# Second stack: last layer 256 columns wide, rotary swap by VectorE shuffle, a gate's minimum taken ahead of its tanh

## The reference, cut to what matters

```
def _hybrid_layer(h, pos, ...):
    proj = h @ w_in                       # 2048 -> 5120
    (c_val, c_glu, c_gate, q, k, v, a_gate, r_x, r_gate) = jnp.split(proj, split_pts, axis=-1)
    c = c_val * sigmoid(c_glu)
    c = causal_depthwise_conv(c, 31 taps); c = silu(layer_norm(c)); c = c @ conv_pw_w + b
    y_conv = c * silu(c_gate)
    q = partial_rotary(q.reshape(B, L, 16, 64), pos)     # 16 heads, first 16 of 64 features
    k = partial_rotary(k.reshape(B, L, 4, 64), pos)      # 4 key heads, 4 query heads for each
    att = sliding_window_sink_attention(q, k, v, sinks)  # window 128, meta keys always seen
    y_attn = att * silu(a_gate)
    r = causal_depthwise_conv(r_x, 4 taps)
    r = rg_lru(r, ...)      # a = exp(-8 sigmoid(r @ wa + ba) softplus(-lam)), scan over tokens
    y_lru = r * silu(r_gate)
    mixed = concatenate([y_conv, y_attn, y_lru]) @ w_out  # 2048 -> 2048
    return layer_norm(alpha * h + mixed)

def _partial_rotary(x, pos):              # half = 8
    rot = concatenate([x1 * cos - x2 * sin, x2 * cos + x1 * sin])
    return concatenate([rot, x[..., 16:]])

second_block: h = layer_norm(concat(meta, x)); two layers; return h[:, 16:]
```

## Time and profile before

| | |
|---|---|
| median of 3 runs | 3391.97 us (3391.57 to 3392.92) |
| profiled execution | 3391.2 us, span 3389.4 us |
| granted TensorE clock, mean | 0.992 |
| busy share of the span | PE 98%, PEld 84%, DVE 58%, ACT 49%, POOL 15% |
| second stack | from about 2457 us to the end; first product of layer 0 at 2485.39 us, of layer 1 at 2932.64 us |

### The profile page before, as it was taken

How to read it: one execution, slowest core, us unless ns; L and a number is a source line. 1 busy time by engine, 2 the same in 40 slices (tenths; PEclk the granted TensorE clock), 3 DMA queues, 4 the chain that set the end, 5 groups by cost and what they waited for, 6 DMA issues and landing times.

```text
span 3389.4 us, 48369 instructions
## 1 busy us (share of the span) xinstructions
PE 3319.6 (98%) x17528; PEld 2838.2 (84%) x17528; DVE 1966.8 (58%) x2190; ACT 1653.5 (49%) x2322; POOL 498.9 (15%) x425
## 2 busy tenths in 40 slices
PE   8999999999999999999999999999979999999998
PEld 7888888888888888888888888888869889898897
DVE  6666645444444556666545444445466776667755
ACT  5444555555444444444555554444335464545643
POOL 4554400000000104554200000000020000010000
PEclk9999999999999999999999999999989999999998
DMA  6555555555555555555554555555533334443342
GB/s 235 173 169 175 183 174 167 168 173 173 193 192 193 199 182 182 170 173 174 175 177 165 169 173 187 193 193 185 180 138 134 116 125 156 156 138 124 124 144 95
DMA packets 157148, 567.24 MB, mean 167 GB/s; under 512 B 17536, under 2 KB 19728, under 8 KB 156752
## 3 DMA queue, kind: packets, MB, share of 16 engines
q1 hardware_dynamic: 155680, 558.00, 49.0%
q0 software_dynamic: 1344, 7.49, 0.6%
HBM read 563.32 MB, written 2.10 MB: 167 GB/s over the span
## 4 chain that ended last, share of the span: by engine, by line
PE 95%; DVE 3%; ACT 1%; POOL 1%; issue 0%; DMA 0%; SPq 0%; ACTq 0%; DVEq 0%; POOLq 0%
PE acc L1506 22%; PE acc L1508 22%; PE acc L1507 22%; PE acc L1757 6%; PE acc L1759 6%; PE acc L1758 6%; PE work L1566 1%; DVE w_lo L965 1%; PE work L1592 1%; PE work L1835 1%; PE work L1836 1%; PE work L1806 1%; PE work L1736 1%; PE work L1737 1%; PE work L1738 1%
## 5 line engine op out<-in xcount | busy, mean ns | idle before, releaser
L965 DVE TENSOR_TENSOR w_lo<-raw,w_hi 128x1024 fp32r<-128x1024 f32 x1056 | 1401.3, 1336 | 1214.4 <-ACT w_hi L565 944.0
L565 ACT ACTIVATE w_hi<-raw 128x1024 fp32r<-128x1024 f32 x832 | 876.4, 1058 | 964.3 <-PE acc L1508 961.9
L1506 PE MATMUL acc<-w_hi,hT_hi 128*128 128x512 f32 x2560 | 1015.2, 397 | 2.3 <-DVE hT_lo L971 2.3
L1508 PE MATMUL acc<-w_hi,hT_lo 128*128 128x512 f32 x2560 | 998.9, 390 | 0.0
L1507 PE MATMUL acc<-w_lo,hT_hi 128*128 128x512 f32 x2560 | 997.5, 390 | 0.0
L1508 PEld LDWEIGHTS acc<-w_hi,hT_lo 128*128 128x128 f32 x2560 | 481.0, 188 | 102.7
L1506 PEld LDWEIGHTS acc<-w_hi,hT_hi 128*128 128x128 f32 x2560 | 481.5, 188 | 97.8 <-issue 2.7
L1507 PEld LDWEIGHTS acc<-w_lo,hT_hi 128*128 128x128 f32 x2560 | 481.8, 188 | 95.8
L579 ACT ACTIVATE w_hi<-raw 128x1024 fp32r<-128x1024 f32 x224 | 236.1, 1056 | 395.8 <-PE acc L1759 381.0
L1757 PE MATMUL acc<-h_hi,w_hi 128*128 128x272 f32 x1152 | 344.7, 299 | 0.0
L1759 PE MATMUL acc<-h_hi,w_lo 128*128 128x272 f32 x1152 | 333.2, 289 | 0.0
(11 more groups left out here) (311 smaller groups left out, 3738.7 us busy)
## 6 DMA issues: line engine op xcount, KB each, us to landing
raw<-weights SPq DMA_DIRECT2D x1056, 512.0 KB, 3.3
mat<-mats POOLq DMA_DIRECT2D x2, 1536.0 KB, 8.1
X<-x_in SPq DMA_DIRECT2D x8, 256.0 KB, 7.9
out<-out_rows SPq DMA_DIRECT2D x8, 256.0 KB, 2.3
par<-params POOLq DMA_DIRECT2D x2, 640.0 KB, 5.4
cst<-consts POOLq DMA_DIRECT2D x1, 872.0 KB, 5.0
cst<-consts POOLq DMA_DIRECT2D x1, 704.0 KB, 4.8
ropeC<-rope POOLq DMA_DIRECT2D x2, 256.0 KB, 5.6
```

The source lines that it names most:

```text
L565: act.activation(w_hi[:, slot, :], raw[:, slot, :], ACT.Copy).then_inc(hi_ready, 1)
L965: dve.tensor_tensor(w_lo[:, s % RING, :], raw[:, s % RING, :], w_hi[:, s % RING, :], ALU.subtract)\
L1506: pe.matmul(o, stat[0][:, kc, token], hi, start=(kc == 0), stop=False)
L1508: ins = pe.matmul(o, stat[1][:, kc, token], hi, start=False, stop=(kc == KC - 1))
```

## The change

1. **Last layer.** `FROM[l]` is 0 for layer 0 and 16 for the last. In the last layer the query tiles, `r_gate`, `a_gate` and `c_gate` tiles (24 of 40), all 16 output tiles and what ACT, DVE, POOL and PE make of them skip the 16 meta columns: 256 instead of 272. Keys, values, the convolution's input and the recurrent part keep 272. The meta tokens' own scores, softmax parts and transposes fall away (`score_parts`).
2. **Rotary swap.** `turn_keys` and `rotate` are gone. DVE swaps features by `stream_shuffle`, which permutes partitions within groups of 32 (`PAIR`); the sign sits in the sine table. Query heads are reordered on the host (`head_pairs`), with the gate columns, output rows and sinks, so that a pair's two heads use the two key heads that already lie on the two halves of a key tile. Keys are now made in one go: a shuffle and three operations of 2 x 272 columns, after g = 14. `turn_values` no longer waits for the keys; the first `scores` does.
3. **Order.** `values` moves from `at` = 6 to `at` = 0 of the next period, directly ahead of `scores`; `copy_o` moves to `at` = 5, ahead of `exps`. `lru_min` runs after g = 44, 48, 52, 56, first in its list, and no longer waits for the tanh; the tanh of b = 0 waits for the minimum instead, and heads ACT's list of its half. `short_conv` stands ahead of the taps of its half.
4. The constants lose the five 128-column matrices: 552 KB in place of 872.

The diff, cut to its core (the left-out lines put `k:TOK` or `FROM[l]:TOK` in place of all columns, and count semaphores anew):

```diff
-E_ID, E_ROT, E_SEL, E_SELROT = 0, P, 2 * P, 4 * P
-E_COS = 6 * P
+FROM = [0] * (DEPTH - 1) + [META]
+PAIR = [i + 8 if i < 8 else i - 8 if i < 16 else i for i in range(32)]
+E_ID = 0
+E_COS = P
...
-        def conv_tap(eng, ch, j):
+        def conv_tap(eng, l, ch, j):
             x, o = PJ[:, CVAL + ch, :], PJ[:, CGLU + ch, :]
             w = R2_DW + CONV_K * ch + CONV_K - 1 - j
+            k = max(j, FROM[l])
             if j == 0:
-                return eng.tensor_scalar(o, x, par2[:, w:w + 1], par2[:, R2_DWB + ch:R2_DWB + ch + 1], ALU.mult, ALU.add)
-            return eng.scalar_tensor_tensor(o[:, j:TOK], x[:, 0:TOK - j], par2[:, w:w + 1], o[:, j:TOK], ALU.mult, ALU.add)
+                return eng.tensor_scalar(o[:, k:TOK], x[:, k:TOK], par2[:, w:w + 1], par2[:, R2_DWB + ch:R2_DWB + ch + 1],
+                                         ALU.mult, ALU.add)
...
+        def of_tokens(l, i):
+            return FROM[l] if QUERY <= i < QUERY + 8 or i >= RGATE else 0
+        def score_parts(l):
+            return ((P, S1, S0), (P, S0, SMETA)) + (() if FROM[l] else ((META, SMETA, S_COLS),))
...
                 act.wait_ge(gate_ready2, 8 * l + n + 1)
                 j, b = n // 2, n % 2
+                if b == 0:
+                    act.wait_ge(gate_min, 4 * l + j + 1)
                 dst = (PJ[:, RX + j, :], IG[:, j, :])[b]
                 act.activation(dst, acc[:, 3, 0:TOK], ACT.Tanh, scale=0.5, bias=hb[:, 4 * b + j:4 * b + j + 1])\
                     .then_inc(gate_tanh2, 1)
...
+                if 45 <= g <= 59 and g % 2:
+                    lru_gate(l, (g - 45) // 2)
                 t = (g - 5) // 2
                 if g % 2 and 4 <= t < 40:
                     copy_tile(l, t)
...
                 c, at = divmod(g - ATT_START, ATT_STEP)
+                if at == 5 and 1 <= c < 9:
+                    copy_o(l, c - 1)
                 if at == 5 and 0 <= c < 8:
                     exps(l, c)
-                if at == 4 and 1 <= c < 9:
-                    copy_o(l, c - 1)
                 if at == 0 and 1 <= c < 9:
                     normalise(l, c - 1)
                 if at == 2 and 1 <= c < 9:
                     copy_pt(l, c - 1)
-                if 45 <= g <= 59 and g % 2:
-                    lru_gate(l, (g - 45) // 2)
...
-            def keys(l, g):
...
-                dve.tensor_tensor(K2[:, g, :], work[:, b, 0:TOK], cst2[:, E_COS:E_COS + TOK], ALU.mult).then_inc(k2_ready, 1)
-                dve.tensor_tensor(rs2[:, :], work[:, b + 1, 0:TOK], cst2[:, E_SIN:E_SIN + TOK], ALU.mult).then_inc(k2_ready, 1)
-                dve.wait_ge(k2_ready, 12 * l + 3 * g + 2)
-                dve.tensor_tensor(K2[:, g, :], K2[:, g, :], rs2[:, :], ALU.add).then_inc(k2_ready, 1)
-                dve.wait_ge(k2_ready, 12 * l + 3 * g + 3)
+            def keys(l):
+                dve.wait_ge(tile_copied, 40 * l + MADE[KEY + 1])
+                x = PJ[:, KEY:KEY + 2, :]
+                cos, sin = (cst2[:, e:e + TOK].unsqueeze(1).to_broadcast([P, 2, TOK]) for e in (E_COS, E_SIN))
+                dve.stream_shuffle(K2[:, :, :], x, PAIR).then_inc(k2_ready, 1)
+                dve.tensor_tensor(Kc[:, :, :], x, cos, ALU.mult).then_inc(k2_ready, 1)
+                dve.wait_ge(k2_ready, 4 * l + 1)
+                dve.tensor_tensor(K2[:, :, :], K2[:, :, :], sin, ALU.mult).then_inc(k2_ready, 1)
+                dve.wait_ge(k2_ready, 4 * l + 3)
+                dve.tensor_tensor(K2[:, :, :], K2[:, :, :], Kc[:, :, :], ALU.add).then_inc(k2_ready, 1)
...
                 n = 8 * l + c + 1
-                dve.wait_ge(q_rotated, n)
+                dve.wait_ge(tile_copied, 40 * l + MADE[QUERY + c])
                 if c:
                     dve.wait_ge(scored2, n - 1)
-                dve.tensor_tensor(Qr[:, :], work[:, 3, 0:TOK], cst2[:, E_SIN:E_SIN + TOK], ALU.mult).then_inc(q_ready, 1)
-                dve.wait_ge(q_ready, 2 * n - 1)
+                k = FROM[l]
+                dve.stream_shuffle(Qr[:, k:TOK], PJ[:, QUERY + c, k:TOK], PAIR).then_inc(q_ready, 1)
+                dve.wait_ge(q_ready, 3 * n - 2)
+                dve.tensor_tensor(Qr[:, k:TOK], Qr[:, k:TOK], cst2[:, E_SIN + k:E_SIN + TOK], ALU.mult).then_inc(q_ready, 1)
+                dve.wait_ge(q_ready, 3 * n - 1)
                 dve.wait_ge(q_cos, n)
-                dve.tensor_tensor(Qr[:, :], Qr[:, :], Qc[:, :], ALU.add).then_inc(q_ready, 1)
+                dve.tensor_tensor(Qr[:, k:TOK], Qr[:, k:TOK], Qc[:, k:TOK], ALU.add).then_inc(q_ready, 1)
...
             def lru_min(l, j):
                 dve.wait_ge(gate_ready2, 8 * l + 2 * j + 1)
-                dve.wait_ge(gate_tanh2, 8 * l + 2 * j + 1)
                 dve.tensor_scalar(PJ[:, j, :], acc[:, 3, 0:TOK], par2[:, R2_BA + j:R2_BA + j + 1], 0.0, ALU.add, ALU.min)\
                     .then_inc(gate_min, 1)
...
+                if g == 14:
+                    keys(l)
                 if g == 17:
                     query(l, 0)
+                if g in (44, 48, 52, 56):
+                    lru_min(l, (g - 44) // 4)
                 c, at = divmod(g - ATT_START, ATT_STEP)
...
+                if g in (38, 42, 44, 48):
+                    short_conv(l, (38, 42, 44, 48).index(g))
                 if 24 <= g < 72:
                     taps = 4 * CONV_K
                     conv_taps(l, taps * (g - 24) // 48, taps * (g - 23) // 48)
-                if g in (38, 42, 44, 48):
-                    short_conv(l, (38, 42, 44, 48).index(g))
-                if g in (45, 49, 53, 57):
-                    lru_min(l, (g - 45) // 4)
...
-            def tile_half(l, k, s, bank, hh, stat):
+            def tile_half(l, k, s, bank, hh, stat, token):
                 pe.wait_ge(split_ready, HALVES * (U2 + UNITS2 * l + k) + s + 1)
-                o = acc[:, bank, 0:TOK]
+                o = acc[:, bank, token:TOK]
                 for kk in range(8):
                     kc = 8 * hh + kk
                     if stat == of_y and kc in (0, 12):
                         pe.wait_ge(y2_lo, 5 * l + (3 if kc == 0 else 5))
                     hi, lo = (w[:, s % RING, P * kk:P * kk + P] for w in (w_hi, w_lo))
-                    x_hi, x_lo = stat(kc)
+                    x_hi, x_lo = (x[:, token:TOK] for x in stat(kc))
                     pe.matmul(o, hi, x_hi, start=(kc == 0), stop=False)
                     pe.matmul(o, hi, x_lo, start=False, stop=False)
                     ins = pe.matmul(o, lo, x_hi, start=False, stop=(kc == KC - 1))
...
-            def turn_keys(l, g):
-                b, e, ch = 2 * (g % 2), g % 2, g // 2
-                if g >= 2:
-                    pe.wait_ge(k2_ready, 12 * l + 3 * (g - 1))
-                pe.matmul(work[:, b, 0:TOK], cst2[:, E_SEL + P * e:E_SEL + P * e + P], PJ[:, ch, :], start=True, stop=True)
-                pe.matmul(work[:, b + 1, 0:TOK], cst2[:, E_SELROT + P * e:E_SELROT + P * e + P], PJ[:, ch, :],
-                          start=True, stop=True).then_inc(kv2_turned, 1)
...
-            def rotate(l, c):
-                pe.wait_ge(tile_copied, 40 * l + MADE[QUERY + c])
+                ins.then_inc(v2_turned, 1)
+            def scores(l, c):
+                pe.wait_ge(q_ready, 3 * (8 * l + c + 1))
                 if c == 0:
-                    pe.wait_ge(k2_ready, 12 * (l + 1))
-                else:
-                    pe.wait_ge(q_ready, 2 * (8 * l + c))
-                pe.matmul(work[:, 3, 0:TOK], cst2[:, E_ROT:E_ROT + P], PJ[:, QUERY + c, :], start=True, stop=True).then_inc(q_rotated, 1)
-            def scores(l, c):
-                pe.wait_ge(q_ready, 2 * (8 * l + c + 1))
-                if c == 0:
+                    pe.wait_ge(k2_ready, 4 * (l + 1))
                     pe.wait_ge(v2_copied, 2 * (l + 1))
-                g = c // 2
                 for a in range(2):
                     half = slice(HD * a, HD * a + HD)
-                    k = K2[half, g, :]
+                    k = K2[half, c // 4, :]
                     o = work[:, 1 + a, :]
                     pe.matmul(o[:, S1:S0], Qr[half, META + P:TOK], k, start=True, stop=True, skip_group_check=True)
-                    pe.matmul(o[:, S0:SMETA], Qr[half, META:META + P], k[:, 0:META + P], start=False, stop=True, skip_group_check=True)
-                    ins = pe.matmul(o[0:META, SMETA:S_COLS], Qr[half, 0:META], k[:, 0:META], start=False, stop=True,
+                    ins = pe.matmul(o[:, S0:SMETA], Qr[half, META:META + P], k[:, 0:META + P], start=False, stop=True,
                                     skip_group_check=True)
+                    if FROM[l] == 0:
+                        ins = pe.matmul(o[0:META, SMETA:S_COLS], Qr[half, 0:META], k[:, 0:META], start=False, stop=True,
+                                        skip_group_check=True)
                 ins.then_inc(scored2, 1)
...
-                if c < 7:
-                    pe.wait_ge(q_ready, 2 * (n + 2))
                 for a in range(2):
```

(31 more changed lines are left out.)

235 lines of the change are left out of this document (125 added, 110 removed).

## The result

| | before | after |
|---|---|---|
| median | 3391.77 us (3390.77 to 3392.92, 4 runs) | 3332.02 us (3331.41 to 3333.60, 4 runs) |
| ratio, 95% interval | | 0.9824 (0.9809 to 0.9839) |
| profiled execution | 3391.2 us, span 3389.4 | 3333.6 us, span 3331.8 |
| layer 0, first product to first product of layer 1 | 447.25 us | 432.12 us |
| layer 1, first product to the end | 456.76 us | 411.71 us |

The gain is 59.8 us where 49.8 were predicted, and the time lies 4 us under the lower end of the range. Beside the last experiments the same kernel took 3331.47 us (3330.78 to 3333.10, 5 runs; ratio 0.9824, 0.9810 to 0.9837).

The account below looks back on a forecast made before the run. PE, busy 98% of the span, was taken as the bound. Savings of 14.7 + 1.7 + 12.1 + 12.9 + 1.6 + 5.4 + 1.4 = 49.8 us gave a median of about 3342.2 us, range 3336 to 3355.

Parts of the forecast that it names:

- swaps removed: PE, both layers: 8 key matmuls and 8 query swaps per layer go, 0.46 us each, saving 14.7 us.
- value-turn wait: PE's wait for DVE's keys before the value turns goes in each layer, 0.86 us each, saving 1.7 us.
- gate stops: PE's eight stops before the gate products go, with the minimum ahead of the tanh: 12.1 us saved.
- 1920 products narrower: Last layer's stream matmuls on PE run 16 columns narrower, 6.7 ns less each: 12.9 us saved.
- plain f32 narrower: Last layer: 59 plain f32 matmuls (value, pointwise, sums, means) lose 16 columns on PE, saving 1.6 us.
- 16x16 scores gone: Last layer: 16 small meta-token score products vanish from PE, priced at 0.14 us each, 2.2 us.
- 16x16 turns gone: Last layer: 16 small turns vanish from PE, 0.11 us each plus 0.09 on the turn ahead, 3.2 us.
- values joined: Value products directly ahead of scores on PE: one stream switch fewer, 14 times at 0.10 us, saving 1.4 us.
- shuffles, on PE's path: DVE's query shuffles, taken as 0.43 us each, hide in 8.3 us free per 7 halves: 0 us.
- the rival's 6 to 12: Rival, chance 0.12: ACT or DVE reaches tanh or minimum late, PE's gate waits return; 6 to 12 us stay, 3348 to 3354.
- The floor under the step: Rival, chance 0.08: weight side sets PE's step below 272 columns; the 12.9 us shrink to 0 to 6, 3349 to 3355.
- The single pass: Rival, chance 0.02: at 256 columns PE's products fall into an almost four times longer mode, 580 us more, about 3930.

## Why the prediction was right and wrong

| step | predicted, us | measured, us | from |
|---|---|---|---|
| swaps removed | 14.7 | 6.7 of 7.1 for the queries put back; key blocks of 1.84 and 1.88 gone in each layer | product put back, trace |
| value-turn wait | 1.7 | wait gone | waits |
| gate stops | 12.1 | 12.7 alone, 24 taken last | two runs |
| 1920 products narrower | 12.9 | 15.0 | step 118.3 against 126.1 ns |
| plain f32 narrower | 1.6 | 1.3 | blocks of the last layer against layer 0; all columns back: 29.8 for the four terms of the narrowing, 19.9 predicted |
| 16x16 scores gone | 2.2 | 9.6 | products put back |
| 16x16 turns gone | 3.2 | 3.4 | turn block 1.50 and 1.08 |
| values joined | 1.4 | 2.7 to 3.0 | blocks, values apart (4.3 with the longer wait) |
| shuffles, on PE's path | 0 | 0 | four shuffles: 0.6, within the scatter |

**The bound and the mechanisms held.** PE set the time, every product taken from it counted in full, and DVE hid the shuffles. The periods of 7 halves in layer 0 became shorter by 0.64 us (28.38 to 27.74) where 0.56 were given: the 0.45 of the swap and 0.19 instead of 0.10 for the switch.

**The step that failed** is the price of the 16x16 scores: "0.14 us, from 2551.62 to 2551.76", read as the distance to the next start. That distance is what the product holds the engine; it isn't what it prevents. The prediction did look for a side effect on the turns (0.09 us on the one ahead) and not for one on the scores, although both heads' products stand in the same rows and use different halves of the array: had nothing parted them, they could have run together. This one term is 7.1 to 7.4 us of the 10 that were missing. The list of rivals held nothing on this side, so the range, drawn down by 6 us only, ended at 3336.

**Two sizes were off.** The line between 272 and 512 gave 6.7 ns for 16 columns; it is 7.8 from the ends of the same stretch, 2.1 us in all. The Trainium skill, "TensorE: Matmul & The Clock Gate", section "Back-to-back issue gap", gives 81 ns at 128 columns and 131 ns at 512, which made an estimate of 4.0 us. The trace disagrees: 226.7 ns at 512 columns, and 0.38 to 0.55 ns a column between 240 and 272 instead of 0.13. The switch between the stream and the plain products is 0.19 to 0.21 us rather than 0.10: only the way in (0.22 in place of 0.126) had been counted. The step behind the way out is long as well, 0.23 us from 2550.80 to the next start at 2551.03. 7.2 for the scores, 2.1 for the step, 1.3 for the switches and 0.2 for the turns make 10.8 and cover the miss of 10.0.

**The rivals.** The gate stops didn't return; the run with the old order shows what that would have been, and at 24 us the rival's 6 to 12 was too small. The floor under the step doesn't exist at 240 columns. The single pass was kept at 256. For the shuffle, the Trainium skill, "VectorE: DVE Perf Modes", section on the perf-mode tier table, led to an estimate of 0.3 to 0.4 us for 272 columns; the trace has 0.46 us.

**What stays open.** Why the 16x16 product parts its neighbours wasn't separated (tiling mode or row group, say). The value products paired and failed to pair within one bank, and each time it failed the shapes differed; no run tries unlike shapes on purpose. Nor was it shown why the clock fell behind one stop of over 2 us and not behind another, or which of DVE's operations makes it stand 1 us later against PE in the attention part; the shuffle isn't a bottleneck there, since four of them cost 0.6 us.

## What to carry to other kernels

Price a product by what the block becomes without it, not by its distance to the next start: look at the halves of the array that its neighbours use, and put products of the same shape that can pair next to each other (rows 0 to 63 with 64 to 127, or columns 0 to 63 with 64 to 127), the small odd ones last. In this kernel that order alone gave 29.2 us with no work removed, half as much as the whole change. A saving in the waits depends on order: the same edit is worth 12.7 us ahead of the others and 24 behind them, so sum waits last, against the shortened stream.
